# Expert blocks of a mixture-of-experts layer: tokens gathered in row quarters and turned by VectorE, slot picking done by the pair

## What is computed

```python
_, idx = lax.top_k(jnp.where(expert_mask, biased, -jnp.inf), TOP_K)        # 8 of 64 experts per token
w = w / jnp.sum(w, axis=-1, keepdims=True) * ROUTED_SCALE
shared = (jax.nn.silu(h @ sh_gate) * (h @ sh_up)) @ sh_down
def run_block(args):
    tok, wt, e = args
    xb = h[tok]
    hid = jax.nn.silu(xb @ w_gate[e]) * (xb @ w_up[e])      # 1024 -> 256
    return (hid @ w_down[e]) * wt[:, None]                  # 256 -> 1024
```

## Time and profile before

| | |
|---|---|
| median of 3 runs | 2153.9 us (2151.55 to 2154.21) |
| the profiled execution: its own time | 2138.5 us |
| its span, first to last instruction | 2136.7 us |
| mean granted PE clock | 0.948 |
| busy: PE, DVE, ACT, POOL | 1835.1, 846.2, 542.0, 426.2 us |
| block loop of the first layer | about 450 to 1146 us |
| block loop of the second layer | about 1546 to 2097 us |

### The profile page before, as it was taken

How to read it: one execution, slowest core, us unless ns; L and a number is a source line. 1 busy time by engine, 2 the same in 40 slices (tenths; PEclk the granted TensorE clock), 3 DMA queues, 4 the chain that set the end, 5 groups by cost and what they waited for, 6 DMA issues and landing times. The chain is left out here.

```text
span 2136.7 us, 39465 instructions
## 1 busy us (share of the span) xinstructions
PE 1835.1 (86%) x11495; PEld 992.2 (46%) x11496; DVE 846.2 (40%) x2836; ACT 542.0 (25%) x1163; POOL 426.2 (20%) x417
## 2 busy tenths in 40 slices
PE   4999699879999999999997589879688887888885
PEld 3545454435445545445553355545444444444442
DVE  2245563363333333333334526543532323223334
ACT  2142352222222222222221214233222222222221
POOL 0001300012223223222321000130122222222220
PEclk8999899999999999999999889969799999999998
DMA  8315510449999789897985853631599999999994
GB/s 278 126 66 201 188 60 1 177 170 377 369 388 357 257 309 359 315 376 270 383 334 198 297 158 110 250 129 34 209 354 370 409 399 411 397 406 400 363 385 185
DMA packets 170400, 578.28 MB, mean 271 GB/s; under 512 B 29756, under 2 KB 34592, under 8 KB 153448
## 3 DMA queue, kind: packets, MB, share of 16 engines
q1 hardware_dynamic: 134592, 515.49, 62.7%
q0 software_dynamic: 29056, 60.07, 7.7%
q10 hardware_dynamic: 6696, 1.98, 0.4%
HBM read 565.73 MB, written 45.75 MB: 286 GB/s over the span
## 5 line engine op out<-in xcount | busy, mean ns | idle before, releaser
L1208 PE MATMUL bank<-arena 128*64 128x256 f32 x5120 | 643.0, 395 | 124.8 <-DMA arena<-in_exp_w_down 81.5
L1208 PEld LDWEIGHTS bank<-arena 128*64 128x64 f32 x5120 | 353.0, 140 | 293.1 <-DMA arena<-in_exp_w_down 86.8
L676 POOL DMA_INDIRECT yrows<-arena x158 | 160.3, 1014 | 832.8 <-ACT arena L907 814.7
L1221 PE MATMUL bank<-arena 128*64 128x512 f32 x1264 | 306.5, 606 | 0.7 <-issue 0.5
L657 POOL DMA_INDIRECT arena<-hrows,arena x164 | 185.9, 1133 | 144.3 <-DVE arena L1650 91.6
L1680 DVE TENSOR_TENSOR arena<-arena,bank 64x256 f32<-64x256 f32 x160 | 68.0, 425 | 353.9 <-ACT arena L891 353.8
L902 ACT ACTIVATE arena<-bank 128x128 f32<-128x128 f32 x158 | 44.2, 280 | 565.6 <-PE bank L1227 565.6
L907 ACT ACTIVATE arena<-bank 128x512 f32<-128x512 f32 x158 | 94.4, 597 | 210.1 <-PE bank L1221 210.1
L973 PE MATMUL bank<-arena 128*128 128x512 f32 (+3 forms) x384 | 133.9, 512 | 11.7 <-DVE arena L1337 11.7
L1645 DVE COPY arena<-bank 128x3 f32<-128x3 f32 x164 | 26.4, 161 | 288.9 <-PE bank L1192 288.3
L1199 PE MATMUL bank<-arena 128*128 128x128 f32 x648 | 121.9, 311 | 7.8 <-DMA arena<-hrows,arena 7.8
(11 more groups left out here) (297 smaller groups left out, 1834.1 us busy)
## 6 DMA issues: line engine op xcount, KB each, us to landing
arena<-in_exp_w_gate SPq DMA_DIRECT2D x128, 1024.0 KB, 8.8
arena<-in_exp_w_up SPq DMA_DIRECT2D x128, 1024.0 KB, 11.1
arena<-in_exp_w_down SPq DMA_DIRECT2D x128, 1024.0 KB, 9.0
arena<-in_w_ada SPq DMA_DIRECT2D x10, 3072.0 KB, 13.7
arena<-yrows SPq DMA_DIRECT2D x24, 1024.0 KB, 16.3
arena<-in_w_ada SPq DMA_DIRECT2D x8, 2048.0 KB, 9.9
arena<-in_w_in SPq DMA_DIRECT2D x8, 2048.0 KB, 18.8
arena<-in_w_out SPq DMA_DIRECT2D x4, 2048.0 KB, 12.1
```

Of the source, the lines that this page charges most:

```text
L676: pool.indirect_dma_start(out=yrows, out_offset=bass.IndirectOffsetOnAxis(ap=SIXS[u], axis=0), in_=YSB[u], in_offset=None, bounds_check=2 ...
L1208: ins = pe.matmul(bank[b_par][64 * gu:64 * gu + 64, 0:HID], XGT[b_par][:, c, hh, :], wv[:, gu, hh, c, :], start=(c8 == 0), stop=(c8 == 7))
L1221: ins = pe.matmul(bank[2 + b_par][64 * cg:64 * cg + 64, :], HIDT[b_par][:, c, :], wv[:, c, cg * 512:(cg + 1) * 512], start=(c == 0), stop= ...
```

## The change

- `hrows` now holds quarters of a row (256 numbers, 1 KB). DVE first writes a reordered copy `HP` of each tile of `H`, and POOL stores that. `YS` shares the memory of `HP`, so ACT waits for the stores (`pool_hr`) ahead of its first write to `YS`.
- A gather is two POOL instructions of 128 rows of 1 KB: partition 32q + s takes quarter q of slot s, the second instruction that of slot 32 + s. One DVE transpose in 32x32 blocks (`turn_tokens` on DVE) then writes `XGT` directly. PE's four transposes and ACT's `xe` are gone. DVE does it right behind `product`.
- `XGT` now has features 8p + c on partition p, so gate and up are loaded with 8 rows (8 KB) to a partition, down in two halves of 4 KB. `up` writes gate and up of one half of the hidden units side by side; SiLU and `product` work on 128x128 instead of 64x256, and `turn_hidden` is one 128x128 transpose.
- Slots are picked for a pair of blocks at once, in four steps: `one_hot`, `meta` on PE, `slots` on DVE, `spread` on PE (a 128x8 product that puts each token number on all four partition groups), then `slot_rows` and `indices` on DVE. PE does `meta` behind `down` of the even block and `spread` behind `down` of the odd one.
- On DVE an odd iteration is now: product, turn, `slot_rows`, `indices`, `one_hot`, and only then the copy to `SIXS`. The gather of block b+4 is issued in iteration b, ahead of the scatter of block b.
- Ahead of the loop the `WK` operations are split around the first two turns. `DG` is made by ACT behind the loop (`a_dg`).

```diff
+        HP = at(rPROJ, NT, DM)
...
-        hrows = nc.dram_tensor("hrows", (2 * (T + 1), 512), F32, kind="Internal").ap()
+        hrows = nc.dram_tensor("hrows", (4 * (T + 1), 256), F32, kind="Internal").ap()
...
-        w = at(ring[k], 2, 2, 4, HID)
+        w = at(ring[k], 2, 8 * HID)
         for j, src in enumerate((eg, eu)):
-            sp.dma_start(w[:, j].rearrange("p h c n -> p h (c n)"),
-                         src[bass.ds(l * NE + e, 1)].rearrange("a (h p c) n -> p (a h) (c n)", h=2, c=4)
+            sp.dma_start(w[:, j], src[bass.ds(l * NE + e, 1)].rearrange("a (p c) n -> p (a c n)", c=8)
                          ).then_inc(sp_land[k], 16)
     def load_down(e, k):
-        sp.dma_start(at(ring[k] + 4096, 2 * DM),
-                     ed[bass.ds(l * NE + e, 1)].rearrange("a (p c) n -> p (a c n)", c=2)).then_inc(sp_land[k], 16)
+        sp.dma_start(at(ring[k] + 4096, 2, DM),
+                     ed[bass.ds(l * NE + e, 1)].rearrange("a (c p) n -> p (a c) n", c=2)).then_inc(sp_land[k], 16)
...
-    hdst = hrows[2:2 * (T + 1), :].rearrange("(t p h) n -> t p (h n)", t=NT, h=2)
+    hdst = hrows[4:4 * (T + 1), :].rearrange("(t p h) n -> t p (h n)", t=NT, h=4)
     for i, t in enumerate(TS):
-        pool.wait_ge(v_h, NT + i + 1)
-        pool.dma_start(hdst[t], H[:, t, :]).then_inc(pool_hr, 16)
+        pool.wait_ge(v_hp, i + 1)
+        pool.dma_start(hdst[t], HP[:, t, :]).then_inc(pool_hr, 16)
     pool.wait_ge(pool_hr, 16 * NTS)
     for k in range(2):
-        pool.dma_start(hrows[k:k + 1, :], X[0:1, 0, 0:512]).then_inc(pool_s[k], 16)
+        pool.dma_start(hrows[2 * k:2 * k + 2, :].rearrange("(a h) n -> a (h n)", a=1), X[0:1, 0, 0:512]).then_inc(pool_s[k], 16)
     def gather(k):
-        pool.indirect_dma_start(out=XG[k], out_offset=None, in_=hrows,
-                                in_offset=bass.IndirectOffsetOnAxis(ap=GIX[k], axis=0),
-                                bounds_check=2 * (T + 1) - 1, oob_is_err=False).then_inc(pool_g[k], 16)
-
-    for b in range(3):
-        pool.wait_ge(v_ix, b + 1)
-        if b >= 2:
-            pool.wait_ge(pe_x, b - 1)
-        gather(b % 2)
+        for h in range(2):
+            pool.indirect_dma_start(out=XG[k][:, 256 * h:256 * h + 256], out_offset=None, in_=hrows,
+                                    in_offset=bass.IndirectOffsetOnAxis(ap=GIX[k][:, h:h + 1], axis=0),
+                                    bounds_check=4 * (T + 1) - 1, oob_is_err=False).then_inc(pool_g[k], 16)
+
+    for j in range(2):
+        for k in range(2):
+            pool.wait_ge(v_ix[k], j + 1)
+            if j:
+                pool.wait_ge(v_xt, k + 1)
+            gather(k)
     pairs = pool.value_load(NPR[0:1, 0:1], min_val=1, max_val=MAXB // 2 + 1)
     with pool.Fori(0, pairs) as i:
         for u in range(2):
-            pool.wait_ge(v_ix, i * 2 + (u + 4))
-            pool.wait_ge(pe_x, i * 2 + (u + 2))
+            pool.wait_ge(v_ix[u], i + 3)
             pool.sem_inc(pool_go, 1)
-            gather((u + 1) % 2)
+            pool.wait_ge(v_xt, i * 2 + (u + 3))
+            pool.sem_inc(pool_go, 1)
+            gather(u)
...
+    act.wait_ge(pool_hr, 16 * NTS)
...
-    def xe(b_par, val):
-        act.wait_ge(pe_x, val)
-        act.activation(XGT[b_par], bank[(4, 6)[b_par]][:, :].rearrange("p (c h s) -> p c h s", c=4, h=2), ACT.Copy).then_inc(a_xe, 1)
-
     def silu(b_par, val, free):
         act.wait_ge(pe_gu, val + 1)
         if free is not None:
             act.wait_ge(v_hid, free)
-        act.activation(HS[64:128, :], bank[b_par][0:64, 0:HID], ACT.Silu).then_inc(a_si, 1)
+        act.activation(HS, bank[b_par][:, 0:P], ACT.Silu).then_inc(a_si, 1)
...
-            act.activation(HIDT[u], bank[5][:, 0:2 * SLOTS].rearrange("p (c s) -> p c s", c=2), ACT.Copy).then_inc(a_h, 1)
+            act.activation(HIDT[u], bank[5][:, 0:P].rearrange("p (c s) -> p c s", c=2), ACT.Copy).then_inc(a_h, 1)
             silu(1 - u, i * 2 + (u + 2), i * 2 + (u + 1))
-            xe(u, i * 2 + (u + 3))
...
+    act.wait_ge(v_wk, 1)
+    for t in TS:
+        for k in range(KV_DVE, TOPK):
+            ins = act.activation(DG[:, t, k - KV_DVE, :], IDENT, ACT.Copy, scale=WK[:, t, k:k + 1])
+    ins.then_inc(a_dg, 1)
...
+    def meta(val_oh, val_vx):
+
         pe.wait_ge(v_oh, val_oh)
+        if val_vx is not None:
+            pe.wait_ge(v_vx, val_vx)
+        for t in TS:
+            ins = pe.matmul(bank[7][:, 0:6], OH[:, t, :], KVP[:, t, :], start=(t == T0), stop=(t == NT - 1))
+        ins.then_inc(pe_meta, 1)
+
+    def spread(val_vx, val_ix):
+        pe.wait_ge(v_vx, val_vx)
         if val_ix is not None:
-            pe.wait_ge(v_ix, val_ix)
-        for t in TS:
-            ins = pe.matmul(bank[7][:, 0:3], OH[b_par][:, t, :], KV[:, t, bass.ds(e, 1), :].rearrange("p a c -> p (a c)"),
-                            start=(t == T0), stop=(t == NT - 1))
-        ins.then_inc(pe_meta, 1)
-
-    def turn_tokens(b_par, val):
-        pe.wait_ge(pool_g[b_par], val)
-        for c in range(4):
-            ins = pe.transpose(bank[(4, 6)[b_par]][:, c * P:(c + 1) * P], XG[b_par][:, c:512:4], IDENT)
-        ins.then_inc(pe_x, 1)
+            pe.wait_ge(v_ix[1], val_ix)
+        pe.matmul(bank[4][:, 0:8], DUP4, VX, start=True, stop=True).then_inc(pe_sp, 1)
...
-        wv = at(ring[k], 2, 2, 4, HID)
-        for c8 in chunks:
-            hh, c = c8 // 4, c8 % 4
-            for gu in range(2):
-                ins = pe.matmul(bank[b_par][64 * gu:64 * gu + 64, 0:HID], XGT[b_par][:, c, hh, :], wv[:, gu, hh, c, :],
-                                start=(c8 == 0), stop=(c8 == 7))
+        wv = at(ring[k], 2, 8, HID)
+        for c in chunks:
+            for nh in range(2):
+                ins = pe.matmul(bank[b_par][64 * nh:64 * nh + 64, 0:HID].rearrange("p (g n) -> p g n", g=2), XGT[b_par][:, c, :],
+                                wv[:, :, c, P * nh:P * nh + P], start=(c == 0), stop=(c == 7))
...
-        for c in range(2):
-            ins = pe.transpose(bank[5][:, c * SLOTS:(c + 1) * SLOTS], HIDB[64:128, c:HID:2], IDENT[64:128, 64:128])
-        ins.then_inc(pe_h, 1)
-
-    meta(0, 0, 1, None)
-    meta(1, 1, 2, 1)
-    for j in range(NTS + 1, 2 * NTS):
-        shared_down(j)
-    turn_tokens(0, 16)
-    meta(0, 2, 3, 2)
-    turn_tokens(1, 16)
+        pe.transpose(bank[5][:, 0:P], HIDB, IDENT).then_inc(pe_h, 1)
+
+    for j in range(3):
+        meta(j + 1, j if j else None)
+        if j < 2:
+            spread(j + 1, j if j else None)
...
+    pe.wait_ge(v_xt, 1)
     for k in range(3):
         with pe.If(e % 3 == k):
             expert_landed(e, k)
             up(0, k, range(8), True)
+    spread(3, 2)
...
-            meta(1 - u, b + 3, b + 4, b + 3)
             slot_now = None if u == 0 else slot
             e = expert_of(b + 1)
             slot = pe.snap(e % 3)
-            pe.wait_ge(a_xe, b + 2)
+            pe.wait_ge(v_xt, b + 2)
...
-            turn_tokens(u, i * 16 + 32)
...
+            if u == 0:
+                meta(i + 4, i + 3)
+            else:
+                spread(i + 4, i + 3)
+
+    pe.wait_ge(a_dg, 1)
...
+        dve.wait_ge(v_h, NT + i + 1)
+        dve.tensor_copy(HP[:, t, :].rearrange("p (q c d) -> p q d c", q=4, c=8),
+                        H[:, t, :].rearrange("p (q d c) -> p q d c", q=4, c=8)).then_inc(v_hp, 1)
...
+    def one_hot(b, val, chain):
+
+        es = [expert_of(b + k) for k in range(2)]
+        if val is not None:
+            dve.wait_ge(pe_meta, val)
+        for k in range(2):
+            chain(dve.tensor_scalar(RR[:, T0:, k:k + 1], GG[:, T0:, bass.ds(es[k], 1)], BASE[:, 0:1], None, ALU.subtract))
+            chain(dve.tensor_copy(KVP[:, T0:, 3 * k:3 * k + 3], KV[:, T0:, bass.ds(es[k], 1), :].rearrange("p t a c -> p t (a c)")))
+        chain(dve.tensor_scalar(BASE, BASE, float(P), None, ALU.add))
+        return dve.tensor_tensor(OH[:, T0:].rearrange("p t (k s) -> p t k s", k=2),
+                                 IOTA.rearrange("p (k s) -> p k s", k=2).unsqueeze(1).broadcast_to([P, NTS, 2, SLOTS]),
+                                 RR[:, T0:].unsqueeze(3).broadcast_to([P, NTS, 2, SLOTS]), ALU.is_equal).then_inc(v_oh, 1)
+
+    def slots(val, val_sp, chain):
+
+        dve.wait_ge(pe_meta, val)
+        if val_sp is not None:
+            dve.wait_ge(pe_sp, val_sp)
+        for k in range(2):
+            chain(dve.tensor_copy(M3[64 * k:64 * k + 64, 0:3], bank[7][64 * k:64 * k + 64, 3 * k:3 * k + 3]))
+        chain(dve.tensor_scalar(VX[:, 0:4], COLS[:, 10:14], TK[:, 1:2], None, ALU.mult))
+        dve.tensor_scalar(VX[:, 4:8], COLS[:, 10:14], TK[:, 2:3], None, ALU.mult).then_inc(v_vx, 1)
+
+    def slot_rows(six, val, chain):
+
+        dve.wait_ge(pe_sp, val)
+        own = bank[4][:, 4:8].rearrange("p (b h) -> p b h", h=2)
+        chain(dve.tensor_scalar(SR, own[:, :, 0], COLS[:, 6:7], COLS[:, 2:3], ALU.mult, ALU.add))
```

(65 more changed lines are left out.)

85 lines of the change are left out of this document (30 added, 55 removed).

## The result

The changed kernel takes 2236.6 us (median of 6 runs, 2233.3 to 2252.6) against 2154.1 (6 runs, 2151.6 to 2157.4): a ratio of 1.0407, 95% interval 1.0382 to 1.0432. It is 4.1% slower, and the prediction had 2107 in 2074 to 2150, with 0.14 for slower.

A forecast was written before the change was run, and what follows sets the result against it. PE was taken to bound the first loop, DMA the second. First loop -49 us, starts +2.5 and +0.5, slow clock +2, second loop -3: -47 from a median of 2153.9, so 2107 us, range 2074 to 2150.

The forecast's parts named there:

- the wait ahead of down: PE's wait for ACT's copy of the turned hidden before down: taken as 0, with 0.65 us as the bound.
- PE's block: PE's time for a first-loop block where nothing waits: from 7.35 to 6.30 us (6.1 to 6.95).
- the ring: DVE's copy to SIXS, scatter, next gather, landing, turn: 13.5 us a pair with a 6.3 us landing, 6.75 a block.
- rival C: Slower: the ring above 14.7 us a pair, landing above 7.5 us; 2180 to about 2200 us; chance 0.13.
- Rival D: More waits put PE at 1.2 GHz often, first loop's mean clock 0.99 to 0.90: 2140 to 2160 us; chance 0.06.
- From the block to the loop: Stepping 92 first-loop blocks with PE and DMA clocks: 69 us saved, 20 back as waits for weights, 49 net.
- rival A: The ring is slack: 6.3 us a block or less, first loop 624 us, total 2090 (2075 at 6.1); chance 0.15.
- second loop: Layer two's block loop, bound by DMA: 5 us saved by stepping, 2 lost to gather rows, -3 us net.
- The start: Work ahead of layer one's loop: first up 7 us later, a 4.3 us wait gone, about +2.5 us.
- Gathers of 1 KB rows: Second loop's DMA cost of smaller gather rows: between nothing and 22 us, taken as 2 us.
- the HP copies, ACT's wait and DG: Work outside the block loops: each taken as 0, the HP copies at most 8 us if their cover is gone.

The follow-up runs named there:

- The pause: POOL clears a spare 128x512 tile twice between each scatter and the gather behind it; on the changed kernel 2179.9 us, on the early copy 2092.5 us.
- early copy: The changed kernel with DVE's copy to SIXS, and its wait for the stores, put back right behind the product in both iterations; 2123.8 us.
- the kernel with the short pause: The early copy with DVE's comparison moved right behind the odd turn and one 128x512 clearing by POOL ahead of each gather; 2068.5 us, the lowest time.
- the extra comparison: The early copy with DVE's comparison moved right behind the odd turn, plus a second, useless comparison at the old place; 2097.3 us.
- the kernel before with quarter gathers: The kernel before the change, with each gather split into two indirect DMAs of 1 KB rows; 2155.4 us, 1.0016 of before.
- the tiny pause: The kernel with the short pause, with POOL's clearing cut from 128x512 to 128x16 elements; 2072.7 us.

## Why the prediction was wrong

**The step that failed is the wait ahead of down.** For PE's block the prediction said of the wait for the hidden copy that it "ends about 0.5 us before up does, so I take 0, with 0.65 as the bound". In the cycle above that copy started 3.8 us after up had ended, and down began 4.5 us late. Over the first loop PE waited 75.3 us for it, in 24 blocks, and 41 of 92 blocks had the copy late. The reason lies in the ring section, which saw the late copy to SIXS and the late scatter, but counted them only as a delay of the next gather. What they also do is to let POOL issue up to six indirect DMAs in a row, and PE's signals to ACT come late in such rows. No term and no rival had that.

**What it costs.** The pause, which frees the signals, takes the changed kernel from 2236.6 to 2179.9 us, 57 less. The signals cost more than that, as far as the pause itself lengthens the ring, by 1.75 us a round. The late signals also turned the ring round: the waits moved from the gather to PE's down and spread.

**The ring** was the right place: order on DVE, the copy to SIXS, the scatter, the gather. Its terms were off both ways. DVE's part takes 5.1 to 6.1 us, not 4.5, and the hand-over to POOL 0.9 us, not 0.1. Against that, the landing was 4.8 us in the mean where the ring bound, not 6.3. So the mean of about 13.5 us without the pause is the predicted 13.5 by luck, and rival C's point, 14.7, is passed in single rounds but not in the mean. With the pause in it, the ring costs 2179.9 - 2092.5 = 87 us against the same kernel with an early copy. No run has the late copy with timely signals and no pause. Taking 1.75 us off for each of the 39 to 45 rounds gives 2101 to 2112 us, an estimate; by it the forecast of 2107 would have held without the late signals, and they would carry more than the whole loss.

**Rival D's clock.** The first loop was at 0.92, and down took 3.68 us where PE had waited. Late signals are not the only waits that go with it: the changed kernel with the pause has none and is at 0.93, the early copy still has 43 late blocks and is at 0.97, as is the kernel with the short pause.

**PE's block**, where nothing waits, was right and came out a little shorter. In the version with the lowest time, a block and the start of the next:

```profile
812.53 2.81 PE L1220 MATMUL bank<-arena 128*64 128x256 f32 x24
815.27 0.33 PE L1238 MATMUL bank<-arena 128*128 128x128 f32 x1
815.53 1.08 PE L1220 MATMUL bank<-arena 128*64 128x256 f32 x8
816.45 1.89 PE L1233 MATMUL bank<-arena 128*64 128x512 f32 x8
818.26 0.39 PE L1213 MATMUL bank<-arena 128*128 128x8 f32 x2
818.58 2.81 PE L1220 MATMUL bank<-arena 128*64 128x256 f32 x24
```

6.05 us from start to start, where the sum had 6.30 (6.1 to 6.95): the four transposes and the issue gap ahead of up are gone, and the turned hidden takes 0.26, as taken (0.25). The turn takes 0.71 us (0.65 predicted).

**From the block to the loop** held as well, once the ring was out. For a slack ring (rival A) the stepping gave 624 us where it gave 692 for before, 68 less. The same version's first loop:

```profile
L1238 PE MATMUL bank<-arena x92: 327/328/457, 471.2 to 1077.4; 128*128 128x128 f32 x92
```

606 us for 677, 71 less, with 35.6 us of waits for weights for 8.1. Its second loop takes 530 us, 8 less (3 predicted), and its whole 2068.5, where rival A said 2090, or 2075 with a block of 6.1. It is not the kernel that was predicted, but it shows what the new PE block is worth once nothing holds it up.

**The start** was under-priced: +2.5 predicted, +8.5 measured to the first turned hidden (+6.5 to +13.5 in the kernels made from it). Up came at 463.62, 13.5 us later than in the earlier trace rows. PE had stood still for 6.9 us ahead of it, and up ran at a granted clock of 0.53 (463 to 470 us), mostly at 1.2 GHz:

```profile
463.62 6.58 PE L1214 MATMUL bank<-arena 128*64 128x256 f32 x32 [6.88 <-DVE arena L1680]
```

**Gathers of 1 KB rows** by themselves: 0 to 7 us in the kernel before, in line with the 2 taken. The costs taken as nothing on the HP copies, ACT's wait and DG were not tried one by one; in the version with the lowest time start, middle and tail together are 7 us longer than before, nearly all of it the start.

## What to carry to other kernels

When an order is changed on an engine with slack, look for what other engines wait for in it, and put small copies that release a transfer first: here one 0.15 us copy, put behind 5 us of work on an engine that is busy for 39%, cost 113 us. When something in an order becomes late, ask what will then be issued together, and not only what waits for it. Price a ring with the hand-overs that rows show between engines (0.9 us from the copy to POOL's issue here, not 0.1), and measure it over all its rounds: the one printed above took 17.1 us, the mean 15.2. Before an experiment is read, look whether it did what it was built for; the extra comparison lengthened no gather. When a wait's named releaser is "remote" or long done, ask what was issued at that moment; one instruction of pause told more here than any reading of the waits.

## What the hardware showed that was not expected

PE's signals can arrive late while its work started in time. In the changed kernel, where POOL issued up to six indirect DMAs 0.3 us apart, the late blocks had ACT's copy start 0.8 to 5.1 us after the transposition's end. It didn't have to wait for the end of the row: in 26 of 41 late blocks ACT started before POOL's last issue had ended, in the other 15 it started 0.2 to 1 us behind it. DVE's chained small operations went on in such stretches at their usual 0.2 to 0.4 us. A row of two issues 0.31 us apart, as in nearly every block of the kernel before, made nothing late. Where the scatter and the gather were 0.4 us or more apart, it nearly vanished as well: 285 us of remote waits in the first loop in the changed kernel, 164 with the early copy, 8 in the kernel before with quarter gathers, 0 with the tiny pause. By what path the signals are delayed is open; no run here separates the descriptors in flight from the act of issuing.

The Trainium skill (Perfetto Trace Analysis, Tensor Engine Instruction) says that a matmul's end in a trace is estimated and that its signal goes out only once PSUM has acknowledged the write. The trace agrees in that such a delay shows in no row of PE. The Trainium skill (SBUF — State Buffer, SBUF: two separate sides) says that PE waits for nobody at SBUF, and GpSimd and DVE exclude each other. The second half agrees with the gather of 1.49 us, though in the kernel before only 21 of the 91 gathers that overlapped a comparison took over 1.3 us. By the first half the delay does not arise at PE's SBUF ports, and no run here shows where it does.
